# Opening and even projection in one program, with the first normalization scaled after the turn to channels

## What is computed

```python
def adaln(cond, w, b):
    return jnp.split(jax.nn.silu(cond) @ w + b, 6, axis=-1)

def modulate(x, g, shift, scale):
    return rmsnorm(x, g) * (1 + scale[:, None]) + shift[:, None]

sh1, sc1, g1, sh2, sc2, g2 = adaln(cond, W['ada_w'][l], W['ada_b'][l])
h = modulate(x, W['norm1_g'][l], sh1, sc1)
z = h @ W['w_in_e'][e]          # 1024 x 2688, then attention and a bidirectional scan
```

## Time and profile before

| | us |
|---|---|
| median of 3 runs | 2938.19 |
| the profiled execution | 2944.82 |
| its span in the trace | 2943.0 |
| TensorE busy | 2658.4 |
| VectorE busy | 1677.2 |
| ScalarE busy | 1475.3 |
| GpSimd busy | 390.7 |
| opening stage, from the start to the projection's first load | 77.6 |
| even projection, to the end of its products and mixing | up to about 261 |

### The profile page before, as it was taken

One profiled execution on the slowest core, in us unless ns is written; L12 is line 12 of the kernel. 1 busy time (PEld: TensorE's weight loads), 2 busy tenths in 40 slices (PEclk: granted clock), 3 DMA queues, 4 the chain that ended last, 5 costly groups with the idle time before them and its releaser, 6 DMA issues. The chain is left out here.

```text
span 2943.0 us, 46503 instructions
## 1 busy us (share of the span) xinstructions
PE 2658.4 (90%) x16139; PEld 2316.4 (79%) x16139; DVE 1677.2 (57%) x2404; ACT 1475.3 (50%) x2301; POOL 390.7 (13%) x521
## 2 busy tenths in 40 slices
PE   3897979999999899998989988888899999999993
PEld 1786967787886588887867768877799999999993
DVE  2145655545555633232241138864788898988886
ACT  1223755555543233332132236651788887878783
POOL 2033211011101220000030024404200000000002
PEclk6997979989999999999999989998899999999997
DMA  8431000000002512222234510031999999999995
GB/s 308 154 122 25 1 6 1 1 1 1 1 2 115 200 48 72 78 71 79 79 107 149 197 69 17 15 110 46 347 386 382 386 380 386 380 382 378 383 378 207
DMA packets 263957, 474.66 MB, mean 161 GB/s; under 512 B 29536, under 2 KB 202720, under 8 KB 257680
## 3 DMA queue, kind: packets, MB, share of 16 engines
q1 hardware_dynamic: 256208, 448.20, 43.2%
q0 software_dynamic: 4416, 14.70, 1.3%
q10 hardware_dynamic: 3200, 9.97, 0.9%
HBM read 456.30 MB, written 16.49 MB: 161 GB/s over the span
## 5 line engine op out<-in xcount | busy, mean ns | idle before, releaser
L3102 DVE TENSOR_TENSOR m_lo<-m_raw,m_hi 128x1408 fp32r<-128x1408 f32 (+1 forms) x459 | 649.3, 1457 | 66.4 <-ACT m_hi L2961 65.7
L2961 ACT ACTIVATE m_hi<-m_raw 128x1408 fp32r<-128x1408 f32 (+1 forms) x459 | 550.8, 1246 | 50.4 <-DMA m_raw<-moe_w_gu 35.6
L213 PE MATMUL acc<-w_hi,h_hi 128*128 128x512 f32 (+1 forms) x1120 | 430.5, 384 | 27.2 <-DVE w_lo L195 13.5
L195 DVE TENSOR_TENSOR w_lo<-w_raw,w_hi 128x1024 fp32r<-128x1024 f32 (+1 forms) x132 | 161.0, 1223 | 491.5 <-ACT w_hi L190 490.7
L215 PE MATMUL acc<-w_hi,h_lo 128*128 128x512 f32 (+1 forms) x1120 | 424.4, 379 | 0.0
L214 PE MATMUL acc<-w_lo,h_hi 128*128 128x512 f32 (+1 forms) x1120 | 424.3, 379 | 0.0
L190 ACT ACTIVATE w_hi<-w_raw 128x1024 fp32r<-128x1024 f32 (+1 forms) x134 | 135.1, 1014 | 468.6 <-PE acc L215 409.0
L213 PEld LDWEIGHTS acc<-w_hi,h_hi 128*128 128x128 f32 x1120 | 212.7, 190 | 81.4 <-issue 23.7
L215 PEld LDWEIGHTS acc<-w_hi,h_lo 128*128 128x128 f32 x1120 | 212.7, 190 | 34.2
L214 PEld LDWEIGHTS acc<-w_lo,h_hi 128*128 128x128 f32 x1120 | 213.0, 190 | 32.5
L2879 PE MATMUL p_gates<-m_hi,x_hi 128*128 128x352 f32 x544 | 181.5, 334 | 5.0 <-DVE m_lo L3102 5.0
(11 more groups left out here) (389 smaller groups left out, 5364.1 us busy)
## 6 DMA issues: line engine op xcount, KB each, us to landing
m_raw<-moe_w_gu SPq DMA_DIRECT2D x544, 352.0 KB
m_raw<-moe_w_dn SPq DMA_DIRECT2D x187, 512.0 KB
ada_w<-ada_w SPq DMA_DIRECT2D x48, 1024.0 KB, 5.9
w_raw<-ffn_w_gu SPq DMA_DIRECT2D x88, 256.0 KB, 2.9
w_raw<-w_in_o SPq DMA_DIRECT2D x24, 512.0 KB, 5.8
w_raw<-ffn_w_dn SPq DMA_DIRECT2D x22, 512.0 KB, 3.6
w_raw<-w_in_e SPq DMA_DIRECT2D x28, 384.0 KB, 3.4
scratch_y_slots<-y_slot ACTq DMA_DIRECT2D x18, 512.0 KB, 6.3
```

The costliest lines, as they stand in the source:

```text
L195: eng.tensor_tensor(lo, self.raw_of(c, k), hi, ALU.subtract).then_inc(self.lo.sem, 1)
L213: eng.matmul(out, hi, whi[:, b, :], start=first, stop=False)
L2961: a.activation(whi[:, u % MSPLIT, 0:size(u)], raw[:, s, 0:size(u)], ACT.Copy).then_inc(s_hi.sem, 1)
L3102: dve.tensor_tensor(wlo[:, u % MSPLIT, 0:n], raw[:, u % MRAW, 0:n], whi[:, u % MSPLIT, 0:n], ALU.subtract).then_inc(s_lo.sem, 1)
```

## The change

`opening_stage` is gone; a class `Opening` holds its work, and the engines do it at the start of `even_project_stage`'s program.

- SyncE loads ident and x first, then seven sets of quad 0, unit 0 of w_in_e, the eighth set, and units 1 to 3.
- Tokens are only scaled by rstd, in place and tile by tile, and turned at once. TensorE turns tile 0 after step 4, tiles 1 and 2 after step 5, tile 3 after step 6, tile 4 after step 7, into `shift_bank`; ScalarE evicts them to `turned_x`.
- Shift and scale stay on the chip. The sums of quad 0 are added to rows that hold the bias (two of each 32 partitions) and the norm's gain (in the others, whose sums are zero); four small matmuls turn these rows to columns, two VectorE operations make gain and shift columns, one value to a channel.
- Each channel block is then scaled and shifted with columns: ScalarE writes h_hi (`block_hi`), VectorE the full value and the rest (`block_lo`), context and latent tokens apart. TensorE waits for each block before its products in the first chunk (`ready`). The work lies between the splits of units 0 to 3 (HI_BLOCKS, LO_BLOCKS).
- w_in_e is read with channel block j on rows 128 j on, which goes with the new order of channels.
- Quad 1 moves into the projection: sixteen steps, behind units 5 to 12 and 17 to 24, with a ring of two sets, two drains and two stores.
- SyncE waits until all tiles are turned ahead of the bias loads, which overwrite x; GpSimd likewise ahead of its memset.

```diff
-    def products(self, eng, c, k):
+    def products(self, eng, c, k, ready=None):
+            if ready is not None:
+                ready(2 * k + b)
             for t in range(NT):
                 mm = self.block(eng, c, k, b, t, whi, wlo)
...
-def opening_stage(K):
...
+    def places(K, ctx):
+        return (K.sb(ctx, "first_w", [P, J, 4 * Opening.CH]), K.sb(ctx, "turned_x", [P, J, T]), K.sb(ctx, "first_squares", [P, D]),
+                K.sb(ctx, "first_rows", [P, Opening.CH]))
...
+    def load_rows(self, eng):
+        for c in range(4):
+            b = self.K.I["ada_b"][0:1, c * self.CH:(c + 1) * self.CH]
+            g = self.K.I["norm1_g"][0:1, c % 2 * self.CH:(c % 2 + 1) * self.CH]
+            at = c * self.COLS
+            eng.dma_start(self.rows[at:at + 2], b.broadcast_to([2, self.CH])).then_inc(self.row_loaded.sem, 16)
+            eng.dma_start(self.rows[at + 2:at + self.COLS], g.broadcast_to([self.COLS - 2, self.CH])).then_inc(self.row_loaded.sem, 16)
...
+    def scale_tile(self, dve, t):
+        x = self.K.x[:, t, :]
+        dve.wait_ge(self.rstd.sem, self.rstd.at(t + 1))
+        dve.tensor_scalar(x, x, self.ss[:, 2, t:t + 1], None, ALU.mult).then_inc(self.scaled.sem, 1)
...
+    def turn_group(self, pe, n):
+        t, half = divmod(n, 2)
+        if half == 0:
+            pe.wait_ge(self.scaled.sem, self.scaled.at(t + 1))
+        if n >= 2:
+
+            pe.wait_ge(self.evicted.sem, self.evicted.at(n - 1))
+        for b in range(4):
+            j = 4 * half + b
+            mm = pe.transpose(self.half_of_bank(n)[:, b * P:(b + 1) * P], self.K.x[:, t, j * P:(j + 1) * P], self.K.ident[:])
+        mm.then_inc(self.turned.sem, 1)
+
+    def evict_group(self, a, n):
+        t, half = divmod(n, 2)
+        a.wait_ge(self.turned.sem, self.turned.at(n + 1))
+        a.activation(self.hat[:, 4 * half:4 * half + 4, t * P:(t + 1) * P], self.half_of_bank(n).rearrange("p (j n) -> p j n", j=4),
+                     ACT.Copy).then_inc(self.evicted.sem, 1)
...
+    def step(self, pe, j):
+        if j == 0:
+            pe.wait_ge(self.mod.widened.sem, self.mod.widened.at(1))
+        pe.wait_ge(self.landed[j].sem, self.landed[j].at(16))
+        for c in range(4):
+            mm = pe.matmul(self.mod.acc[self.mod.part(c), 0, :], self.mod.wide[:, j, :], self.w[:, j, c * self.CH:(c + 1) * self.CH],
+                           start=j == 0, stop=j == J - 1)
+        if j == J - 1:
+            mm.then_inc(self.summed.sem, 1)
+
+    def drain(self, dve):
+        dve.wait_ge(self.row_loaded.sem, self.row_loaded.at(128))
+        dve.wait_ge(self.summed.sem, self.summed.at(1))
+        dve.tensor_tensor(self.rows[:], self.mod.acc[:, 0, :], self.rows[:], ALU.add).then_inc(self.row.sem, 1)
+
+    def turn_rows(self, pe):
+        chosen = self.K.ident[:].rearrange("p (c n) -> p c n", c=4)[:, :, 0:3]
+        pe.wait_ge(self.evicted.sem, self.evicted.at(2 * NT))
+        pe.wait_ge(self.row.sem, self.row.at(1))
+        for q in range(4):
+            mm = pe.matmul(self.bank[:, 12 * q:12 * q + 12], self.rows[:, q * P:(q + 1) * P], chosen, start=True, stop=True)
+        mm.then_inc(self.col.sem, 1)
+
+    def gains(self, dve):
+        dve.wait_ge(self.col.sem, self.col.at(1))
+        dve.tensor_copy(self.cols[:].rearrange("p (c q) r -> p q c r", c=4), self.bank[:, 0:48].rearrange("p (q c r) -> p q c r", q=4, c=4)).then_inc(self.copied.sem, 1)
+        dve.wait_ge(self.copied.sem, self.copied.at(1))
+        cols = self.cols[:, J:2 * J]
+        dve.scalar_tensor_tensor(self.gain[:], cols[:, :, 0:2], 1.0, cols[:, :, 2:3].broadcast_to([P, J, 2]), ALU.add, ALU.mult).then_inc(self.gained.sem, 1)
+
+    def rows_of(self, j):
+
+        return [(slice(0, P) if r == 0 else slice(P, T), self.gain[:, j, r:r + 1], self.cols[:, j, r:r + 1]) for r in range(2)]
+
+    def block_hi(self, a, j):
+        if j == 0:
+            a.wait_ge(self.gained.sem, self.gained.at(1))
+        for at, gain, shift in self.rows_of(j):
+            a.activation(self.K.h_hi[:, j, at], self.hat[:, j, at], ACT.Identity, bias=shift, scale=gain).then_inc(self.hi.sem, 1)
+
+    def block_lo(self, dve, j):
+        if j == 0:
+            dve.wait_ge(self.gained.sem, self.gained.at(1))
+            dve.wait_ge(self.evicted.sem, self.evicted.at(2 * NT))
+        for at, gain, shift in self.rows_of(j):
+            dve.tensor_scalar(self.tokens[:, j, at], self.hat[:, j, at], gain, shift, ALU.mult, ALU.add).then_inc(self.token.sem, 1)
+        dve.wait_ge(self.token.sem, self.token.at(2 * j + 2))
+        dve.wait_ge(self.hi.sem, self.hi.at(2 * j + 2))
+        dve.tensor_tensor(self.K.h_lo[:, j, :], self.tokens[:, j, :], self.K.h_hi[:, j, :], ALU.subtract).then_inc(self.lo.sem, 1)
+
+    def ready(self, pe, j):
+        pe.wait_ge(self.lo.sem, self.lo.at(j + 1))
...
-def even_project_stage(K, z, zs, kc, vc):
+def even_project_stage(K, z, zs, kc, vc, places):
...
-        w = rows_by_partition(I["w_in_e"][0])
+        w = rows_by_block(I["w_in_e"][0])
...
-        mod = Modulation(K, ctx, 8, 1, 2, 1, bias=xf[:, at:at + 512].rearrange("p (m n) -> p m n", m=1))
+        mod = Modulation(K, ctx, 4, 2, 2, 1, bias=xf[:, at:at + 2 * 512].rearrange("p (m n) -> p m n", m=2))
         bank = K.ps(ctx, "shift_bank", [P, 1024])
+        first = Opening(K, ctx, places, mod, bank)
...
-        STEPS = {UNITS + 1 + 2 * n: n for n in range(J)}
-        DRAINS = {UNITS + 1 + 2 * J + 2: 0}
-        LOADS = {UNITS - 1: (0, 1)} | {UNITS + 3 + 2 * n: (n,) for n in range(2, J)}
+        STEP = [UNITS + 1 + n + n // J * UNITS for n in range(2 * J)]
+        STEPS = {u: n for n, u in enumerate(STEP)}
+        DRAINS = {STEP[J - 1] + 3: 0, STEP[2 * J - 1] + 3: 1}
+        LOADS = {UNITS - 1: (0, 1)} | {u + 5: (n + 2,) for n, u in enumerate(STEP[:-2])}
+
+        HI_BLOCKS = {2: range(0, 6), 3: range(6, J)}
+        LO_BLOCKS = {1: range(0, 2), 2: range(2, 6), 3: range(6, J)}
...
+                first.load_tokens(sp)
+                for n in range(J - 1):
+                    first.load_set(sp, n)
                 for c in range(CHUNKS):
                     for k in range(UNITS):
                         g.load(sp, c, k)
+                        if c == 0 and k == 0:
+                            first.load_set(sp, J - 1)
...
+                            first.wait_turned(sp)
                             mod.load_bias(sp)
                         for n in LOADS.get(c * UNITS + k, ()):
-                            mod.load_set(sp, 0, n)
-                mod.store(sp, 0)
+                            mod.load_set(sp, *divmod(n, J))
+                for m in range(2):
+                    mod.store(sp, m)
...
                     if u in STEPS:
-                        mod.products(pe, 0, (STEPS[u],))
-                units(pe, g.products, behind)
+                        m, n = divmod(STEPS[u], J)
+                        mod.products(pe, m, (n,))
+
+                def products(eng, c, k):
+                    if c == 0:
+                        g.products(eng, c, k, lambda j: first.ready(eng, j))
+                    else:
+                        g.products(eng, c, k)
+                for n in range(J):
+                    first.step(pe, n)
+                    if 3 <= n < J - 1:
+                        for t in ((0,), (1, 2), (3,), (4,))[n - 3]:
+                            first.turn_group(pe, 2 * t)
+                            first.turn_group(pe, 2 * t + 1)
+                first.turn_rows(pe)
+                units(pe, products, behind)
...
-                units(a, g.split_hi, behind)
+
+                def split(eng, c, k):
+                    for j in HI_BLOCKS.get(k, ()) if c == 0 else ():
+                        first.block_hi(eng, j)
+                    g.split_hi(eng, c, k)
+                first.load_conditions(a)
+                first.load_rows(a)
+                first.silu(a)
+                for t in range(NT):
+                    first.square_tile(a, t)
+                for n in range(2 * NT):
+                    first.evict_group(a, n)
+                units(a, split, behind)
 
             @block.gpsimd
             def _(pool):
...
-                units(dve, g.split_lo, behind)
+
+                def split(eng, c, k):
+                    for j in LO_BLOCKS.get(k, ()) if c == 0 else ():
+                        first.block_lo(eng, j)
+                    g.split_lo(eng, c, k)
+                    if c == 0 and k == 0:
+                        first.drain(eng)
+                        first.gains(eng)
+                for t in range(NT):
+                    first.scale_tile(dve, t)
+                units(dve, split, behind)
...
-            opening_stage(K)
+
+            with ExitStack() as opening:
+                places = Opening.places(K, opening)
...
-                    even_project_stage(K, z, zs, kc, vc)
+                    even_project_stage(K, z, zs, kc, vc, places)
+                    K.retire("open_")
```

(16 more changed lines are left out.)

59 lines of the change are left out of this document (added).

## The result

The changed kernel takes 2906.41 us (median of six runs, 2905.15 to 2918.31), the kernel before 2940.03 (six runs, 2930.11 to 2946.98). The ratio is 0.9889, with a 95% interval of 0.9871 to 0.9907: faster by 1.1%, some 33 us. Forecast was 2902.1, range 2892 to 2914.

A forecast was written before the change was run, and what follows sets the result against it. TensorE, busy 90% of the span, was taken as the bound, so time is won where it idles or is slow: -40.0 - 3.5 - 1.4 + 8.8 = -36.1 us, giving 2902.1 us from the median 2938.2, range 2892 to 2914.

The forecast's parts named there:

- First product: Opening, up to the even projection's first product: it would start at 43.0 us instead of 82.96, -40.0 us.
- The floor of 41.3: Opening: earliest start of the first product, 41.3 us, if everything follows the DMA alone.
- The clock rival: Opening: TensorE stays at the lower clock through steps and turns, +6.1 us, whole time 2908.2; chance 17%.
- The eight blocks and the table load: Start of projection: scaling blocks cost nothing (at most 2 us uncovered); ScalarE's possible table load 0, at most 1.3 us.
- The hole at unit 4: Projection, fifth unit of w_in_e: TensorE's wait closes, -3.5 us, and the slow stretch behind it goes, -1.4 us.
- the term for the doubled bias: Loads ahead of the fifth unit of w_in_e: 0.26 MB more bias adds 0.6 us.
- the rival that the hole stays: Projection, fifth unit: small packets start later or TensorE comes earlier, +4.9 us, whole time 2907.0; chance 12%.
- The clock's part: Projection, behind the fifth unit: the slow-clock stretch of 13 matmuls following the wait disappears, -1.4 us.
- The steps: Projection: the second quad's eight steps move in at 1.10 us each, +8.8 us (8.0 to 9.4).
- The slower rival: Projection: SyncE held at refills, w_in_e late in 14 units, 69 us, whole time 2971; chance 5%.

The follow-up runs named there:

- the second pair of traces: Kernel before and changed kernel each profiled once more with no edit: 2943.51 us (ratio to before 1.0008) and 2912.66 us (0.9884).
- the kernel with all three edits: Changed kernel with steps where TensorE waits, small loads behind unit 6, and the drain ahead of unit 0's split: 2898.42 us, ratio to before 0.9855.
- e2_turn_late: Changed kernel with all five tiles turned behind the eighth step instead of beside the set loads: 2915.27 us, ratio to before 0.9907.
- the kernel with one quad: Changed kernel without the second quad, only eight steps in the projection and bias loads at their old size: 2896.20 us, ratio to before 0.9838.
- e1_after_again: Changed kernel run and traced once more, no edit: 2912.66 us, ratio to before 0.9884.
- e4_steps_in_waits: Changed kernel with the second eight steps behind units 15, 17, 19, 21, 23, 25, 27, 28, each ahead of the transposes: 2899.44 us, ratio to before 0.9859.

## Why the prediction was right, point by point

**First product** (forecast 43.0, measured 41.71 and 41.95): right within 1.3. The eighth set was there at 34.8 (35.0). The one term that was off is the clock, which rose sooner: after a first tile from 25.68 the step at 27.28 already took 1.06 us, where I kept the lower level until 29.3. So the last tile was done at 34.8 instead of 36.3 and the eighth step at 35.94 instead of 37.3. The chain behind it held: small matmuls 1.03 (0.9), columns 0.5 with their gaps (0.5), block 0 2.1 (2.0). The split of unit 0 stood ahead of the drain, as said, and VectorE started the drain at 37.13 (38.8). That is -41.3 for -40.0 (-40.1 in the second pair of traces). The floor of 41.3 "if everything follows the DMA alone" was too high: the kernel with all three edits reached 40.33.

I had taken the lower level for steps alone from one trace. It isn't fixed. In the second trace of the kernel before, the steps at 31.83 and 34.33 took 1.06 us, and in the changed kernel the third step was fast before any tile was turned, and the fourth took 1.94 again:

```profile
21.31 1.07 PE L755 MATMUL ada<-first_w,cond_wide 128*32 128x512 f32 x8 [0.83 <-DMA first_w<-ada_w]
```

**The clock rival** fell: from 27 to 36 the changed kernel ran at 1.00. That the steps between the tiles can bring the clock up alone is seen above, so this doesn't judge the transposes; forty of them in a row took it from 0.50 to full in `e2_turn_late`. By the Trainium skill, TensorE: Matmul & The Clock Gate, Part 4: PE-mode transpose, they don't count as busy in the same way. The trace of that run doesn't agree; the page gives its times for bf16, and these are fp32.

**The eight blocks and the table load**: TensorE didn't wait for a block after the first, and ScalarE's only table load up to 60 us is the first, at 6.59. Nothing was paid for either, as forecast.

**The hole at unit 4** (-3.5 and -1.4 forecast) is where the working failed: the term for the doubled bias was too small. TensorE came there at 65.4, close to the 65.7 forecast, but the data came late: the split began at 64.49 instead of 61.8. The small packets ahead of it weren't the reason. SyncE issued unit 4's load at 54.0, and the forecast's own sum puts it at 53.6 (61.8 less the 0.6, and less the 7.6 us that the kernel before took from issue to split). What took longer is the way from the issue to the split, 10.5 us.

```profile
64.49 0.85 ACT L190 ACTIVATE w_hi<-w_raw 128x768 fp32r<-128x768 f32 x1 [8.56 <-DMA w_raw<-w_in_e]
...
66.38 0.45 PE L213 MATMUL acc<-w_hi,h_hi 128*128 128x384 f32 x1 [1.00 <-DVE w_lo L195]
```

The DMA issues say why, KB each and median us to landing, of the changed kernel

```profile
ada_w<-ada_w SPq DMA_DIRECT2D x2, 1024.0 KB, 8.9
...
x<-ada_b SPq DMA_DIRECT2D x4, 128.0 KB, 3.3
```

and of the kernel before

```profile
ada_w<-ada_w SPq DMA_DIRECT2D x2, 1024.0 KB, 6.0
...
x<-ada_b SPq DMA_DIRECT2D x4, 64.0 KB, 2.5
```

I priced the doubling of the bias by its extra bytes at 420 GB/s, 0.6 us. Measured against the kernel with one quad it costs 1.6 to 3.0, and the sets behind it landed after 8.9 us in place of 6.0 (6.0 again in the kernel with one quad). So a wait of 1.0 (1.8 in the second execution) was left of 3.5: the rival that the hole stays, at 12%, came in part. From first product to unit 4 the gain was 1.6 instead of 3.5. Of the missing 1.9, 1.0 is that wait, and 0.9 is that TensorE stayed at the lower level for 5.6 us at its start, 3.4 before.

The clock's part came true in one execution and not in the other. In the changed kernel's first trace, after the wait of 1.0:

```profile
67.00:70.00 3.00, 3.00 (x20) 3.00 (x19) 0.96 (x1) 0.97 (x2) 0.00 (x0) 1.00 0.48 131
...
70.00:74.00 4.00, 4.00 (x25) 4.00 (x24) 0.96 (x1) 0.85 (x1) 0.00 (x0) 1.00 0.37 98
```

and in its second, after 1.81:

```profile
67.00:70.00 3.00, 2.52 (x10) 2.53 (x11) 1.33 (x2) 2.06 (x5) 0.00 (x0) 0.71 0.44 125
...
70.00:74.00 4.00, 4.00 (x20) 4.00 (x19) 0.05 (x1) 0.00 (x0) 0.00 (x0) 0.79 0.38 110
```

At 0.71 and 0.79, 30 matmuls in 7 us stand against 45. From unit 4's first product to the split of unit 6 it took 7.2 us instead of 5.6, which is 1.6 for the clock (-1.4 was forecast for having it back). This, the wait (0.8 longer) and the first product (0.2 later) make the 2.8 us between the two attentions. The waits of the stage in the first trace:

```profile
PE shift_bank L930 <- ACT x L974: 10.0, 7, 2.2
...
PE acc L213 <- DVE w_lo L195: 1.0, 1, 1.0
```

**The steps** (+8.8 forecast): +9.7. The term was mis-sized, the mechanism was right: 1.22 us a step. I had read the interval between two products and left out that the matmuls behind it also start a little slow: in the kernel before the next one begins 0.28 us behind the product at 122.43, where 0.17 is usual.

**Sum.** Up to the attention in the first pair of traces: -41.3 to the first product, -1.6 to unit 4, -1.6 to unit 6 (whose split begins at 71.95, before at 116.39: here the clock no longer falls), +9.7 for the steps: -34.7 (from unrounded times), forecast -36.1. So the closeness owes something to luck: the opening came 1.3 better than forecast, and unit 4 and the steps 2.6 worse. In the second pair the same marks give -30.8; there the changed kernel lost the clock behind unit 4 again. The later stages added 5.0 in the first pair and took 0.6 away in the second, so no part of that is shown to come from the change. By the ratios of the timed runs, 0.9889 and 0.9884 in the second set, the gain is 32.6 and 34.1 us, 3.5 and 2.0 short of the forecast.

**The slower rival** (w_in_e late at each refill) didn't come: besides unit 4 TensorE waited for no split, with fourteen refills.

## What to carry to other kernels

Work that waits for a scale and a shift can often be split: do what needs only the data (here squares, scaling by rstd and the turn) beside the loads, and bring the scale in as a column behind the turn; that made 46 us of chain into 6. Put side work of the bounding engine into that engine's own waits before counting what it costs elsewhere: of eight steps, four that stood ahead of the instruction that waits and one behind the last product were free or nearly so. And look at what else sits in the same queue ahead of a load that ends on the path; half a megabyte of broadcast rows cost about 4 us there, some three times what its bytes say at 420 GB/s (1.25 us).

## What the runs showed of the hardware that I had not expected

At unit 4 a wait of 1.0 us left TensorE's granted clock at full speed, waits of 1.8 and 1.9 us were followed by some microseconds near half speed (`e1_after_again`, `e4_steps_in_waits`); so a wait below two microseconds cost itself in one case and about twice itself in the others. The length of one wait doesn't settle it, though: in the changed kernel's first trace a wait of 1.33 us at 196.5 left the clock at 1.00, and two of 1.33 and 0.95 close together, at 222.9 and 224.6, were followed by 0.63 and 0.50. With broadcast rows of 2 KB just ahead in the queue the DMA ran at 285 GB/s, with none at 430. And a stage that no edit touches, the recurrence, took 477 to 487 us from execution to execution, its granted clock between 0.96 and 0.94: a level that no kernel here controlled. What sets it stays open.
